# A decoder layer with product-key experts: selection in alternating chains, the first scatter between other work, and the sample's chain moved to the last passes

## What is computed

```python
q = (xb @ w_q).reshape(PEER_BLOCK, PEER_HEADS, 2, PEER_DK_HALF)
s = jnp.einsum('thcd,hcnd->thcn', q, keys)
sv, si = lax.top_k(s, PEER_TOPK)                       # 16 of 128 keys, on two sides
cand = sv[:, :, 0, :, None] + sv[:, :, 1, None, :]     # 16 x 16 sums
cv, ci = lax.top_k(cand.reshape(...), PEER_TOPK)       # 16 of 256
eid = i0 * PEER_N_KEYS + i1                            # the 128 experts of a token
act = gelu(einsum('td,thkd->thk', xb, w_down[eid]))
out = einsum('thk,thkd->td', softmax(cv) * act, w_up[eid])
```

## Time and profile before

| | us |
|---|---|
| median of 3 runs | 3515.72 (3501.64 to 3517.16) |
| the profiled execution | 3514.68 |
| its span | 3512.9 |
| PE busy in it | 3152.1 |
| DVE busy in it | 2615.6 |

### The profile page before, as it was taken

How to read it: one execution, slowest core, us unless ns; L and a number is a source line. 1 busy time by engine, 2 the same in 40 slices (tenths; PEclk the granted TensorE clock), 3 DMA queues, 4 the chain that set the end, 5 groups by cost and what they waited for, 6 DMA issues and landing times.

```text
span 3512.9 us, 33177 instructions
## 1 busy us (share of the span) xinstructions
PE 3152.1 (90%) x11349; PEld 1837.6 (52%) x11349; DVE 2615.6 (74%) x5082; ACT 773.4 (22%) x2004; POOL 1632.5 (46%) x1269
## 2 busy tenths in 40 slices
PE   8998898987979987755889999999999999999977
PEld 5766777756737652442444543544544544543422
DVE  2397336877878787686699999999999975876640
ACT  2002542213210111250340420430430420420000
POOL 0000002443444677553356665665665764765520
PEclk9999999998987998857999999999999999999999
DMA  4111556887798999977899999999999999999997
GB/s 133 36 36 67 179 180 238 303 318 261 267 339 284 361 386 397 360 248 280 301 360 384 350 356 395 345 371 386 335 382 385 334 395 370 367 376 410 409 358 222
DMA packets 328859, 1077.16 MB, mean 307 GB/s; under 512 B 40524, under 2 KB 76941, under 8 KB 328028
## 3 DMA queue, kind: packets, MB, share of 16 engines
q0 software_dynamic: 172416, 625.03, 47.4%
q1 hardware_dynamic: 121515, 428.89, 33.4%
q10 hardware_dynamic: 34760, 21.14, 1.9%
HBM read 1052.50 MB, written 23.94 MB: 306 GB/s over the span
## 4 chain that ended last, share of the span: by engine, by line
PE 37%; DMA 21%; DVE 18%; issue 9%; POOL 4%; ACT 2%; ACTq 1%; DVEq 0%; POOLq 0%
PE psum L1526 27%; DMA arena<-in_w_up 13%; DVE arena L1780 7%; DMA arena<-in_w_down,arena 4%; POOL arena L1282 3%; PE psum L1519 3%; DVE arena L1798 2%; PE psum L1488 2%; DMA arena<-in_w_q 2%; PE psum L1365 1%; ACTq L2010 1%; PE psum L1367 1%; PE psum L1465 1%; DVE arena L1741 1%; DVE arena L1743 1%
## 5 line engine op out<-in xcount | busy, mean ns | idle before, releaser
L1282 POOL DMA_INDIRECT arena<-in_w_down,arena x1024 | 1419.9, 1387 | 1004.8 <-DVE arena L1780 763.2
L1526 PE MATMUL psum<-arena 128*128 128x512 f32 x3584 | 1628.9, 602 | 95.0 <-DMA arena<-in_w_up 91.0
L1780 DVE CUSTOM_DVE_ANT_0 arena<-arena 128x1024 f32<-128x1024 f32 x1024 | 1214.8, 1221 | 172.7 <-DMA arena<-in_w_down,arena 165.9
L1526 PEld LDWEIGHTS psum<-arena 128*128 128x128 f32 x3584 | 655.8, 192 | 925.2 <-issue 662.0
L1365 PE MATMUL psum<-arena 128*128 128x256 f32 (+2 forms) x1536 | 367.1, 394 | 27.6 <-DVE arena L1681 16.6
L2075 ACT ACTIVATE arena<-arena 128x128 f32<-128x128 f32 x896 | 285.7, 390 | 373.2 <-DVE arena L1798 370.2
L1798 DVE TENSOR_TENSOR arena<-constants,arena 128x1024 f32<-128x1024 f32 x224 | 272.0, 1221 | 108.1 <-ACT arena L2064 57.5
L1519 PEld LDWEIGHTS psum<-arena 128*128 128x128 f32 x1792 | 255.3, 209 | 181.2 <-ACT arena L2075 105.3
L1519 PE MATMUL psum<-arena 128*128 128x128 f32 x1792 | 265.1, 297 | 78.8 <-ACT arena L2075 78.7
L1365 PEld LDWEIGHTS psum<-arena 128*128 128x128 f32 x1536 | 272.6, 198 | 111.9 <-DVE arena L1681 18.9
L284 PE MATMUL psum<-arena 128*128 128x344 f32 x816 | 238.4, 455 | 3.0 <-DVE arena L324 3.0
(11 more groups left out here) (253 smaller groups left out, 2184.8 us busy)
## 6 DMA issues: line engine op xcount, KB each, us to landing
arena<-in_w_up SPq DMA_DIRECT2D x512, 512.0 KB, 6.7
arena<-in_w_gates SPq DMA_DIRECT2D x96, 768.0 KB, 5.7
arena<-in_w_o SPq DMA_DIRECT2D x40, 512.0 KB, 6.7
arena<-in_w_q SPq DMA_DIRECT2D x32, 512.0 KB, 5.8
arena<-in_w_down,arena POOLq DMA_INDIRECT x1024, 8.1
arena<-in_w_chunks SPq DMA_DIRECT2D x26, 512.0 KB, 3.5
arena<-scratch_s POOLq DMA_DIRECT2D x64, 128.0 KB, 7.2
arena<-in_xT SPq DMA_DIRECT2D x4, 1032.0 KB, 7.8
```

Source lines behind the costliest of these rows:

```text
L1282: pool.indirect_dma_start(dst, None, table, bass.IndirectOffsetOnAxis(ap=idN[:, min(n, NT - 1) % 2, j:j + 1], axis=0)).then_inc(here, 16)
L1526: mm = pe.matmul(psum[:, 2 * (m % 2) + h, :], coef_block(m, s % NKEYS), wup[:, s % WUPR, h * 512:(h + 1) * 512], start=first, stop=end)
L1780: dve.tensor_tensor_reduce(row, row, rowD[slot_of["x", n]], 1.0, 0.0, ALU.mult, ALU.add, dots[:, n % 3, j:j + 1]).then_inc(row_used, 1)
```

## The change

Five things change, and with them the planner's figures.

1. `head_keys` runs the two sides of a head as two chains in turns: an instruction waits only for the one of its own side. Where the plan has a head's "ids" and the next head's "keys" one after the other, `ids_and_keys` runs both as chains in turns, with two sets of `sv` and `si`. The plan has 39 such places, 25 keys alone and 25 ids alone. The plan's cost for keys falls from 3.7 to 2.8, that of a joined pair is 1.6 less than its parts, and keys are planned no earlier than 4.5 after the keys before.
2. Seven more row buffers, open for a stretch each, all before row 366.
3. Block 0's turn is an item ("ids0") among the last group's pairs, and its 32 batches follow parts of the last items (`woven`): one after each of the 16 parts of the two output sets, two after turn 5 and two after turn 6, one after each of the 8 parts of the queries, and one after each of the four score items of XS and 5. They use bank 4, and so the items behind the last pair take banks 0, 2 and 6 in turns, three instead of four. Their dense coefficients go to other places, in four copies a batch instead of two. ACT has "hot" and "sevac" as separate entries of the plan.
4. The sample's lists stay at the start of pass 0, but its gathers of `w_down` wait for the end of pass 5, its copies of x are fetched at step 38 of pass 6, and its product on PE stands before step 56 of pass 7.
5. The planner now places the sums of blocks 5 and 6 itself, where its model has the passes end, instead of behind everything.

```diff
-        COST = {"dot": 1.15, "keys": 3.7, "ids": 5.75, ...
+        COST = {"dot": 1.15, "keys": 2.8, "ids": 5.75, ...
+                if kind == "ids":
+                    return n < 3 or m.done("turned", n - 3)
+                return not at or m.end[HALF_HEADS[at - 2]] + 4.5 <= m.now
...
+        woven = {}
+        for k in range(last_pair[3] + 1, NI):
+            if opens_set(k):
+                woven.update({(k, i): 1 for i in range(KD)})
+            elif items[k] in (("turn", 5), ("turn", 6)):
+                woven[k, 0] = 2
+            elif items[k][0] == "query":
+                woven.update({(k, i): 1 for i in range(2)})
+            elif items[k] in scores([XS, 5]):
+                woven[k, 0] = 1
...
-        rows_at = [48704, 49728, 50752, 11328, 37888] + [25600 + D * i for i in range(4)] + [46144] + [8256 + D * i for i in range(3)]
+        rows_at = [48704, 49728, 50752, 11328, 37888] + [25600 + D * i for i in range(4)] + [46144] + [8256 + D * i for i in range(3)] + \
+            [32768, 33792, 34816, 35840, 36864, 35840, 36864]
...
-        while dot_next < SLOTS * (NT + 1) or sum_next < DENSE - 2 or norms_due or sample_at < len(SAMPLE):
+        while dot_next < SLOTS * (NT + 1) or not last_put or norms_due or sum_next < DENSE - 1 or sample_at < len(SAMPLE):
-            if sum_next < DENSE - 2 and m.end.get(("passeded", sum_next + 1), m.now + 1) <= m.now:
+            if sum_next < DENSE and m.end.get(("passeded", sum_next + 1), m.now + 1) <= m.now:
-        plan = m.plan + [("last",)] + [(kind, t) for t in (DENSE - 2, DENSE - 1) for kind in ("sum", "norm")]
+        plan = m.plan + [(kind, t) for t in range(sum_next, DENSE) for kind in ("sum", "norm")]
...
-                turn(0)
-                for q in range(NBATCH):
-                    scatter(0, q)
...
+                        if i == SUP_AT and n == DENSE:
+                            pe.wait_ge(y_sum, DENSE - 1)
+                            pe.wait_ge(smask, NB + 1)
+                            pe.wait_ge(rowS_here, 16 * 2 * NB)
...
+                    a0 = step(dve.max(v[:, 0, 0:8], scur[:, 0, :]))
+                    a1 = step(dve.max(v[:, 1, 0:8], scur[:, 1, :]))
+                    need(a0)
+                    b0 = step(dve.max_index(x[:, 0, 0:8], v[:, 0, 0:8], scur[:, 0, :]))
+                    need(a1)
+                    b1 = step(dve.max_index(x[:, 1, 0:8], v[:, 1, 0:8], scur[:, 1, :]))
```

More of the change, by code:

```diff
@@ L1020, in build_kernel @@
                 continue
+            if sevac_next < NBATCH and m.done("scated", sevac_next):
+                m.put("sevac", sevac_next)
+                m.end["sevaced", sevac_next] = m.on_act(m.now, 1.7)
+                sevac_next += 1
+                continue
+            if dot_next == SLOTS * (NT + 1) and not last_put and m.end["up", SLOTS - 1] + 3.0 <= m.now:
+                m.put("last")
+                last_put = True
+                continue
             if gnorms < shifts and m.end["shift", gnorms] + 2.5 <= m.now:
@@ L1264, in fetch @@
                         pool.wait_ge(row_used, c)
+                    if fill[f] == 1 and slot_of[f] in XB0 + XB12 + XB3 + XB4:
+                        us = (0,) if slot_of[f] in XB0 else (1, 2) if slot_of[f] in XB12 else (3, 4)
+                        for u in us:
+                            pool.wait_ge(copied, copy_no[items.index(("turn", u))] + 1)
+                            pool.wait_ge(xb_out[u % 2], 16 * (u // 2 + 1))
+                    if fill[f] == 1 and slot_of[f] in BIAS0:
+                        pool.wait_ge(pre_done, 2)
                     if fill[f] == 1 and slot_of[f] in LATE:
@@ L1330, in slot_free, with turn, scatter, weave @@
                         pe.wait_ge(copied, copy_no[p] + 1)
+                def turn(n):
+                    pe.wait_ge(picked, head_done(n, HEADS - 1))
+                    pe.wait_ge(coef_done, n + 1)
+                    for c in range(2):
+                        pe.transpose(psum[:, 6, c * P:(c + 1) * P], pick[:, n % 3, c].rearrange("p h k -> p (h k)"), ident)
+                    pe.transpose(psum[:, 6, 2 * P:3 * P], dots[:, n % 3, :], ident).then_inc(turned, 1)
+                def scatter(n, q):
+                    g = NBATCH * n + q
+                    pair = (hot if n else hot0)[:, g % 2]
+                    pe.wait_ge(hot_ready, g + 1)
+                    if g >= 2:
+                        pe.wait_ge(scat_copied, g - 1)
+                    else:
+                        released(last_there)
+                    for t in range(BATCH):
+                        mm = pe.matmul(psum[:, 4 + g % 2, t * P:(t + 1) * P], pair[:, 1, t, :], pair[:, 0, t, :],
+                                       start=True, stop=True)
+                    mm.then_inc(scat_done, 1)
+                scattered = [0]
+                def weave(k, part):
+                    for _ in range(woven.get((k, part), 0)):
+                        scatter(0, scattered[0])
+                        scattered[0] += 1
                 def load_here(k, part):
@@ L1677, in gate_and_add @@
                         dve.wait_ge(row_used, drained[EARLY[1]])
-                    value = psum[:, 2 * (k % 4) + 1, :]
+                    if g == group_of(3) and not br:
+                        dve.wait_ge(row_used, max(drained[q] for q in BIAS0))
+                    value = psum[:, bank[k] + 1, :]
                     sig = gsig[:, i % 2, :]
@@ L1878, in _ @@
                 dve.wait_ge(bias_ready, 3)
-                for s in plan:
+                with_ids = None
+                for s, after in zip(plan, plan[1:] + [("end",)]):
                     if s[0] == "amax":
@@ L1893, in _ @@
                         residual_norm(s[1])
-                    elif s[0] == "keys":
+                    elif s[0] == "ids" and after[0] == "keys":
+                        ids_and_keys(s[1], s[2])
+                        with_ids = after
+                    elif s[0] == "keys" and s != with_ids:
                         head_keys(s[1], s[2])
```

557 lines of the change are left out of this document (377 added, 180 removed).

## The result

The changed kernel takes 3485.35 us (median of 9 runs, 3473.1 to 3497.41) against 3515.07 before (9 runs, 3498.8 to 3521.96). The ratio is 0.9918, 95% interval 0.99 to 0.9936: faster by 30 us or 0.8%. The forecast was 3461 with a range of 3425 to 3505.

What follows compares the result with a forecast made beforehand. TensorE was taken as the bound from 1820 to 3348 us, with room elsewhere. From a span of 3512.9: -10 - 80 - 29 + 0 + 5 + 59.5 = -54.5, a span of 3458 and a median of 3461 us; range 3425 to 3505.

Steps and rivals of the forecast that it cites:

- the likeliest case: Whole kernel: the terms hold as summed, with an own range of 3435 to 3490 us; chance 0.55.
- (a): Start to 1305.9 us: chained selections free VectorE, and TensorE gets back part of its waits; -10 us, bounds 0 and -35.
- (b): Last items and block 0's scatter, 1322.3 to 1610.0 us: weaving the batches into the items saves 80 us.
- waits below 1 us: Sign for the woven batches: the scatter's products stand among the outputs with waits this short.
- The rival that batches keep their pace of 3.85 us: Woven batches hold TensorE as long as before: +73 us, 3534 in all; chance 0.08.
- (c): Pass 0: block 1's first batch comes 81 us after the start, paced by VectorE's list; -29 us, bounds 0 and -42.
- (d): Passes 1 to 6: TensorE is the bound and VectorE is not waited for; 0 us, bounds +-10.
- (e): Pass 7: row gathers share the DMA and the sample's product fills TensorE's free time; +5 us, bounds -5 and +15.
- (f): Tail behind pass 7: 43 row sums stand behind block 6's sum, 67.3 us against 7.7; +59.5 us.
- Tail rows at 2.04 us: Tail: landing, not transfer, sets the row sums' pace; +31 us, 3492 in all; chance 0.12.
- Chains that save nothing: VectorE's selections: MAX8 and its kin start only after the one before ends; 3481 us in all; chance 0.10.
- All waits before 1310 given back: Before 1310 us: TensorE regains all its waits on VectorE, making (a) -39; 3432 us in all; chance 0.12.

Runs made afterwards that it cites:

- the six traces: The changed kernel's first trace and five more with the same program up to pass 6; the last outputs start between 1294.0 and 1310.3 us.
- the last experiment: Changed kernel with five added row buffers nearly closed, four sums and norms behind block 7's rows, x fetched one a step, product in eight parts: 3424.08 us, ratio 0.9754.

## Why the prediction was right, and where it was mis-sized

The sign, the range and the likeliest case's own range (3435 to 3490) hold. The point is 24 us too low: 17 us on the traced spans, and the rest is that the traced execution is faster than the median. The 17 us are less than the single misses, of which two cancel in part, -15.3 in passes 1 to 5 and +18.7 in pass 6. That is luck.

**(a), -10, measured -16.9** (-12 to -28 over the six traces). Right in kind: the chains do it, since with the waits back the outputs start at 1320.7, later than in any of the six.

**(b), -80, measured -78.4** (-61 to -78 over the six traces). The total is right in the first trace and too large for the others, and its mechanism is off. I had the woven batches hold TensorE for 17 us beyond their own products; they wait 45.8 us for ScalarE's scaling, in 12 places, 8.8 us the longest, and the scaling in turn waits 92.5 us for VectorE's comparisons. The prediction named waits below 1 us there as its sign, and a batch that waits several us as a sign that it falls: by that sign the mechanism of (b) failed, and the total came out in spite of it. What balanced it I can only argue: the old waits of that stretch (15.2, 8.7 and 9.4 us) are now 9.4, 0.7 and none, since batches lie over them. The rival that batches keep their pace of 3.85 us would have had 90 us of such waits: it was half true, and the change still paid. The run without weaving bears out the main part, 43 to 60 us of it.

**(c), -29, measured -23.4.** The first batch of block 1 comes 90.4 us behind the pass's start; I had 81. The step that failed is that VectorE's list sets this time. TensorE's waits from 1514.7 to 1605.1, and one of VectorE's in the same stretch:

```profile
PE psum L1659 <- DMA arena<-in_w_up: 21.1, 13, 4.1
DVE arena L2036 <- ACT arena L2320: 11.6, 1, 11.6
```

VectorE is done with its list at 1588.0, 73 us behind the start, and then stands for 11.6 us until block 1's turn comes out of PSUM (L2320). That turn stands before step 30, which TensorE reaches only after 84 us, where I had 68: it waits 21.1 us for pieces of the weights. At the batch itself it waits for nothing. Before the change it was TensorE's path too, as the run without the product shows, where it is worth 12 to 16 us.

**(d), 0, measured -15.3 and +18.7.** The step "PE is the bound and DVE isn't waited for" failed twice, in opposite directions. Passes 1 to 5 were waiting a little for batches: before, the batches of the next block wait 7.1 us for their scaling, which VectorE's comparisons feed; in the changed kernel they wait for none, and with the waits of the selection back it is 7.6 us. The remaining 8 of the 15.3 us are within what the six traces differ by. In pass 6 I had written that the fetches of x stand "in front of pieces of which three lie ready", and left it there. Eight fetches of 512 KB against three pieces in store is 4 MB at 410 GB/s, 10 us, and the burst makes it 21. That PE was the bound there was half of the truth: the earlier trace rows has the DMA at 405 GB/s and a share of 1.02 in that pass, with nothing left for 4 MB more. This is the largest miss.

**(e), +5, measured +19.6.** The term was mis-sized by the sample's product: I let it fill 30 us of idle time that I had counted over the whole pass, and around step 56 there are about 2 us in eight steps. It costs 13.3. The other 6 are in steps 0 to 24 (72.5 us for 65.4), beside the gathers, which the +5 had.

**(f), +59.5, measured +58.3.** Right in every part: 43 rows, 1.32 us each, tail 66.1 against 67.3.

**The rivals.** Tail rows at 2.04 us: fell. Chains that save nothing: fell, with 2.5 us a pair. All waits before 1310 given back: went half the way (17 of 39 us).

Of the 38 us by which passes 6 and 7 grew and the 58 of the tail, the last experiment gets back 10 + 58 and pays 32 for the rows (207.1 against 175.0 in pass 7).

## What to carry to other kernels

Where a program's order is fixed by a model, look in the trace for an engine that stands at one entry while the entries behind it are ready: here one list put 43 rows, 57 us of work, behind waits of 112 and 12 us that need not have come first. Idle time counted over a stage is no room where the work is put: pass 7 had 32 us of it, but only about 2 in the eight steps around the product, and 2.5 of 13.3 us were hidden. A stage in which the DMA is full pays for every fetch that is moved into it, however busy TensorE is. And what lets work run ahead (row buffers) can let a planner put it in front of work with a deadline: with two joined pairs of head searches more among the woven batches that stage took 17 to 34 us longer.

## What was unexpected of the hardware

An operation on VectorE whose inputs are done starts before the end of the one before it, also among MAX8 and FIND_INDEX8: 0.20 us behind the start of one of 0.29. With a wait for the neighbour the start is 0.33 behind the earlier trace rows. Over 22 instructions that made 6.66 us of 9.15.

A gather of 512 KB beside the weight stream costs the weights 0.67 us, though at the 410 GB/s that the DMA reached it would take 1.28 alone. Without gathers the steps of pass 7 take 2.15 us (17.2 for eight) and the DMA moves 245 to 258 GB/s in steps 24 to 48. A piece lands 4.4 us after it is asked for (median), and it is asked for two steps, 4.3 us, ahead of its use. So it seems to be the landing that paces the pass there, and the gathers take first what the stream leaves of the DMA.
